# Narrow input columns of two mixers as four-group fp32 products, step sizes with tokens on the partitions

## What is computed

```
n = rmsnorm(h, norm_mix_w)
proj = n @ w_in                      # 1024 x (2*256 + 512 + 16 + 512 + 512 + 768 + 8)
q, k, v, gate_lr, g_out, z, xbc, dt_raw = split_cols(proj)
# gla: log_a = log_sigmoid(gate_lr @ w_gate2 + b_gate) / 16, sums over chunks of 64 tokens
# ssd: dt = softplus(dt_raw + dt_bias);  a = dt * -exp(a_log)
#      a_cum = cumsum(a) over chunks of 128 tokens; 8 heads
```

## Time and profile before

| | before |
|---|---|
| median of 3 runs | 2532.28 us (2531.97 to 2532.74) |
| the profiled execution's own time | 2532.24 us |
| its span, first to last instruction | 2530.5 us |
| TensorE busy | 2520.5 us of the span |
| DVE, ACT, POOL busy | 1617.3, 1035.7, 1002.1 us |

### The profile page before, as it was taken

How to read it: one execution, slowest core, us unless ns; L and a number is a source line. 1 busy time by engine, 2 the same in 40 slices (tenths; PEclk the granted TensorE clock), 3 DMA queues, 4 the chain that set the end, 5 groups by cost and what they waited for, 6 DMA issues and landing times.

```text
span 2530.5 us, 35784 instructions
## 1 busy us (share of the span) xinstructions
PE 2520.5 (100%) x13674; PEld 2196.4 (87%) x13674; DVE 1617.3 (64%) x3033; ACT 1035.7 (41%) x1621; POOL 1002.1 (40%) x545
## 2 busy tenths in 40 slices
PE   9999999999999999999999999999999999999999
PEld 7789899999999988888888888888889877988888
DVE  6746989899999978888888656610216275730112
ACT  6644344444444433333333534522324365542332
POOL 3324344535555523333332054444441424254442
PEclk9999999999999999999999999999999999999999
DMA  4313255789999999999999332223322322232331
GB/s 157 128 59 109 92 154 161 220 271 359 393 404 405 327 325 343 360 349 350 356 345 348 131 113 87 92 92 100 96 96 74 126 84 69 74 117 92 99 100 59
DMA packets 192907, 488.35 MB, mean 193 GB/s; under 512 B 18505, under 2 KB 83929, under 8 KB 192481
## 3 DMA queue, kind: packets, MB, share of 16 engines
q1 hardware_dynamic: 155872, 351.83, 41.6%
q0 software_dynamic: 36864, 134.23, 14.1%
HBM read 442.98 MB, written 42.88 MB: 192 GB/s over the span
## 4 chain that ended last, share of the span: by engine, by line
PE 91%; DVE 5%; DMA 2%; ACT 1%; POOL 1%; issue 1%; SPq 0%; DVEq 0%; ACTq 0%; POOLq 0%
PE ps L311 29%; PE ps L313 28%; PE ps L312 28%; PE ps L1750 1%; DVE wl L300 1%; DMA tmpb<-in_un,idx 1%; DMA rsb<-in_un,idx 1%; PE ps L2771 1%; PE ps L2868 1%; PE ps L1560 1%; PE ps L2831 1%; DVE tmpb L1879 1%; PE ps L525 0%; POOL wl L300 0%; ACT wh L292 0%
## 5 line engine op out<-in xcount | busy, mean ns | idle before, releaser
L292 ACT ACTIVATE wh<-wraw 128x1024 fp32r<-128x1024 f32 x487 | 514.0, 1058 | 1172.3 <-PE ps L313 1162.4
L300 POOL TENSOR_TENSOR wl<-wraw,wh 128x1024 fp32r<-128x1024 f32 x253 | 618.0, 2450 | 940.5 <-ACT wh L292 823.4
L311 PE MATMUL ps<-Xh,wh 128*128 128x384 f32 (+2 forms) x2336 | 828.9, 355 | 2.6 <-POOL wl L300 0.8
L313 PE MATMUL ps<-Xh,wl 128*128 128x384 f32 (+2 forms) x2336 | 817.5, 350 | 0.0
L312 PE MATMUL ps<-Xl,wh 128*128 128x384 f32 (+2 forms) x2336 | 817.2, 350 | 0.0
L311 PEld LDWEIGHTS ps<-Xh,wh 128*128 128x128 f32 x2336 | 439.7, 188 | 46.3 <-issue 5.5
L313 PEld LDWEIGHTS ps<-Xh,wl 128*128 128x128 f32 x2336 | 439.6, 188 | 38.7
L312 PEld LDWEIGHTS ps<-Xl,wh 128*128 128x128 f32 x2336 | 440.2, 188 | 36.2
L300 DVE TENSOR_TENSOR wl<-wraw,wh 128x1024 fp32r<-128x1024 f32 x234 | 286.0, 1223 | 82.2 <-ACT wh L292 78.9
L311 PE MATMUL ps<-wh,Hh 128*128 128x512 f32 x768 | 299.0, 389 | 0.0
L313 PE MATMUL ps<-wh,Hl 128*128 128x512 f32 x768 | 298.8, 389 | 0.0
(11 more groups left out here) (328 smaller groups left out, 3010.2 us busy)
## 6 DMA issues: line engine op xcount, KB each, us to landing
wraw<-in_uT SPq DMA_DIRECT2D x128, 512.0 KB
wraw<-in_v SPq DMA_DIRECT2D x128, 512.0 KB
wraw<-in_up SPq DMA_DIRECT2D x128, 512.0 KB
gA_scratch<-gl SPq DMA_DIRECT2D x122, 192.0 KB
gl<-gA_scratch SPq DMA_DIRECT2D x122, 192.0 KB
gG_scratch<-gbuf SPq DMA_DIRECT2D x64, 256.0 KB
lg<-gG_scratch SPq DMA_DIRECT2D x64, 256.0 KB
wraw<-in_w_q SPq DMA_DIRECT2D x24, 512.0 KB
```

Source lines behind the costliest of these rows:

```text
L292: act.activation(wh[:, n % 4, :], wraw[:, n % 4, :], ACT.Copy).then_inc(s_wh, 1)
L300: pool.tensor_tensor(wl[:, n % 4, :], wraw[:, n % 4, :], wh[:, n % 4, :].bitcast(F32), ALU.subtract).then_inc(s_wl, 1)
L311: pe.matmul(o, ah, bh, start=start, stop=False)
L313: return pe.matmul(o, al, bh, start=False, stop=stop)
```

## The change

- The narrow tile leaves the weights (`w_in` has one tile less, so that all tile numbers fall by one). Its 24 columns, padded to 32, come as a table `w_misc` of 128 x 256 with 16 more columns for the bias and a_log. POOL multiplies it by the norm's weight (`wm`). `misc_pe` makes 8 plain fp32 products of 32 columns against `hT`, chunk kc into partitions 32 (kc % 4) and following of bank 0: four column groups, each with two chunks. Two of them come among the first products, six after tile 3.
- The four groups are added in the next product: `w_gate2` is laid out four times (128 x 256), so that the gate product over 128 partitions sums them; `sel` is the identity's columns summed over the groups, so that `dt_pe` sums them and turns dt_raw at once to 128 tokens by 4 x 8.
- The chain of the step sizes runs on 128 x 32 elements. Running sums are products with a triangular matrix, the chunk totals one with ones (`decay_sums_pe`); the 4 scans, 8 transposes and the broadcast product go.
- The start is reordered: x in parts of 1, 1, 3, 3 chunks, the first ahead of `vec`, the first weight tile split in halves, 10 products of ones in place of 19.
- The order changes: project(4) stands between `root_pe` and `spread_pe`, project(5) right behind it, then `dt_pe` and the gate products; `decay_sums_pe` stands between tiles 7 and 8. In ACT's loop of six, split 9+i stands ahead of `silu_act(i)` where it stood behind `conv_act(i+2)`.

```
-    w2 = dg[:, 0:256]
+    w2, sel = dg[:, 0:256], dg[:, 256:264]
+    wm = Ss[:, 0, :].rearrange("p (c m) -> p c m", m=32)
+    y = dtt[:, :, :]
+    adt = GE[:, 2, 32:64]
     def in_sp(sp):
+        for i, (lo, hi) in enumerate(X_PARTS):
+            sp.dma_start(hT[:, lo:hi, :], xt[:, lo:hi, :]).then_inc(s_x[i], 16)
+            if i == 0:
+                sp.dma_start(vec[:, :], A["vec"]).then_inc(s_vec, 16)
+                load_w(sp, 0)
+            if i == 1:
+                load_w(sp, 1)
+                sp.dma_start(Ss[:, 0:2, :]..., A["w_misc"]).then_inc(s_small, 16)
+                load_w(sp, 2)
         load_w(sp, 3)
+        sp.wait_ge(s_small, 16)
+        sp.dma_start(w2, A["w_gate2"]).then_inc(s_small, 16)
-        sp.wait_ge(s_dt, 12)
-        sp.dma_start(acD, acT).then_inc(s_acd, 16)
+        sp.wait_ge(s_sd, 1)
+        sp.dma_start(acD32, acT_[:, :]).then_inc(s_acd, 16)
     def in_pool(pool):
+        pool.wait_ge(s_vec, 16)
+        pool.wait_ge(s_small, 16)
+        pool.tensor_tensor(wm, wm, mix, ALU.mult).then_inc(s_const, 1)
+    def misc_pe(pe, kcs):
+        for kc in kcs:
+            j = 32 * (kc % 4)
+            pe.wait_ge(s_x[X_PART[kc]], 16)
+            mm = pe.matmul(ps[B_INA[0]][j:j + 32, :], wm[:, kc, :], hT[:, kc, :], start=kc < 4, stop=kc >= 4)
+        return mm
+    def dt_pe(pe):
+        pe.wait_ge(s_in, 1)
+        for tc in range(4):
+            mm = pe.matmul(ps[6][:, tc * 8:tc * 8 + 8], misc[:, tc * 128:(tc + 1) * 128], sel, start=True, stop=True)
+        mm.then_inc(s_mp, 1)
+    def decay_sums_pe(pe):
+        pe.wait_ge(s_dt, 8)
+        b, by_tok = AUX["sp"], adt.rearrange("p (h c) -> p c h", c=4)
+        bank_free(pe, b)
+        pe.matmul(ps[b][0:32, 128:256], adt, tri[:, :], start=True, stop=True)
+        pe.matmul(ps[b][:, 0:32], tri[:, :], by_tok, start=True, stop=True).then_inc(s_sp, 1)
+        b = AUX["acl"]
+        pe.matmul(ps[b][:, 0:32], ones[:, :], by_tok, start=True, stop=True).then_inc(s_sp, 1)
     def in_pe(pe):
-        for i in range(19):
+        for i in range(10):
             pe.matmul(ps[7][:, 0:128], ones[:, :], ones[:, :], start=True, stop=True)
-        for c, gs in ((0, (0, 1)), (1, (0, 1)), (0, (2,)), (1, (2,)), *((c, (0, 1, 2)) for c in range(2, 8))):
+        for c, gs in ((0, (1,)), (1, (1,)), (0, ()), (0, (2,)), (1, (2,)), (0, (3,)), (1, (3,)), *((c, (1, 2, 3)) for c in range(2, 8))):
+            if not gs:
+                misc_pe(pe, MISC_FIRST)
+        misc_pe(pe, MISC_REST).then_inc(s_mp, 1)
+        freed[B_INA[0]] = done_in(0)
         root_pe(pe, "in", 5)
-        project(3)
+        project(4)
         spread_pe(pe, "in", 6, (s_kept, 1))
-        project(4)
-        ...
         project(5)
+        dt_pe(pe)
+        gate_lr_pe(pe)
         project(6)
         project(7)
+        decay_sums_pe(pe)
         project(8)
-        turn_dt_pe(pe)
         project(9)
         project(10)
-        last_sums_pe(pe)
         turn_b_pe(pe)
     def in_act(act):
             if c == 0:
-                split_hi(act, 0)
+                act.activation(wh[:, 0, 0:512], wraw[:, 0, 0:512], ACT.Copy).then_inc(s_w0, 1)
+                act.activation(wh[:, 0, 512:1024], wraw[:, 0, 512:1024], ACT.Copy).then_inc(s_wh, 1)
         for i in range(6):
+            if i < 4:
+                split_hi(act, 9 + i)
             silu_act(act, i)
             if i < 4:
                 conv_act(act, i + 2)
-                split_hi(act, 10 + i)
     def in_dve(dve):
+        dve.wait_ge(s_mp, 1)
         scaled(dve, misc, B_INA[0])
-        dve.tensor_scalar(y, y, col("dtb", 0, 0, 8), None, ALU.add).then_inc(s_dt, 1)
         xbc_dve(dve, 0)
         xbc_dve(dve, 1)
+        dve.wait_ge(s_mp, 2)
+        dve.tensor_tensor(y, ps[6][:, 0:32]..., dtb..., ALU.add).then_inc(s_dt, 1)
         dve.wait_ge(s_dta, 2)
         dve.tensor_scalar(u1, z, 1.0, None, ALU.add).then_inc(s_dt, 1)
         conv_dve(dve, 0)
         ...
-        dve.tensor_scalar(z, y, ea1[:, 0:1], -1.0, ALU.mult, ALU.mult).then_inc(s_dt, 1)
-        for c in range(4):
-            dve.tensor_tensor_scan(acT[:, cs], ones[0:8, :], z[:, cs], 0.0, ALU.mult, ALU.add).then_inc(s_dt, 1)
+        dve.scalar_tensor_tensor(out=adt..., in0=y, scalar=-1.0, in1=ea1..., op0=ALU.mult, op1=ALU.mult).then_inc(s_dt, 1)
         conv_dve(dve, 1)
         xbc_dve(dve, 3)
+        dve.wait_ge(s_sp, 1)
+        dve.tensor_copy(acT_[:, :], ps[AUX["sp"]][0:32, 128:256]).then_inc(s_sd, 1)
+        dve.tensor_copy(act_[:, :, :], ps[AUX["sp"]][:, 0:32]...).then_inc(s_sd, 1)
```

More of the change, by code:

```diff
@@ L129, in build_program @@
     zs = sb("zs", [128, 4, T], scope=mixer)
-    acT_ = sb("acT", [8, T], scope=mixer)
-    ea1 = sb("ea1", [8, 1], scope=mixer)
+    acT_ = sb("acT", [32, 128], scope=mixer)
+    ea1 = sb("ea1", [128, 8], scope=mixer)
     tri = sb("tri", [128, 128], scope=mixer)
@@ L672, in in_sp @@
     def in_sp(sp):
-        sp.dma_start(vec[:, :], A["vec"]).then_inc(s_vec, 16)
-        for i in range(4):
+        for i, (lo, hi) in enumerate(X_PARTS):
[3 more added lines that the diff above has]
+                load_w(sp, 0)
             if i == 1:
-                for n in range(3):
-                    load_w(sp, n)
-            sp.dma_start(hT[:, 2 * i:2 * i + 2, :], xt[:, 2 * i:2 * i + 2, :]).then_inc(s_x[i], 16)
+                load_w(sp, 1)
+                sp.dma_start(Ss[:, 0:2, :].rearrange("p a t -> p (a t)")[:, 0:272], A["w_misc"]).then_inc(s_small, 16)
+                load_w(sp, 2)
         load_w(sp, 3)
-        sp.dma_start(w2[32:48, :], A["w_gate2"]).then_inc(s_w2, 16)
-        for n in range(4, 13):
+        sp.wait_ge(s_small, 16)
+        sp.dma_start(w2, A["w_gate2"]).then_inc(s_small, 16)
+        for n in range(4, 12):
             load_w(sp, n)
-        sp.wait_ge(s_dt, 12)
-        sp.dma_start(acD, acT).then_inc(s_acd, 16)
+        sp.wait_ge(s_sd, 1)
+        sp.dma_start(acD32, acT_[:, :]).then_inc(s_acd, 16)
         sp.wait_ge(s_acd, ACD[0])
@@ L690, in in_sp @@
             lt_load(sp, h)
-        for n in range(13, 19):
+        for n in range(12, 18):
             load_w(sp, n)
@@ L697, in in_sp @@
             lt_load(sp, 2 * m + 1)
-            load_w(sp, 17 + m)
-        for n in range(21, W_OUT + 4):
+            load_w(sp, 16 + m)
+        for n in range(20, W_OUT + 4):
             load_w(sp, n)
     def in_pool(pool):
+        pool.wait_ge(s_vec, 16)
+        pool.wait_ge(s_small, 16)
+        mix = vec[:, COLS["mix"]:COLS["mix"] + 8].unsqueeze(2).to_broadcast([128, 8, 32])
+        pool.tensor_tensor(wm, wm, mix, ALU.mult).then_inc(s_const, 1)
         masks_pool(pool)
-        for n in range(4, 11):
+        pool.wait_ge(s_const, C_IDENT)
+        pool.tensor_tensor(sel, ident[:, 0:8], ident[:, 32:40], ALU.add).then_inc(s_const, 1)
+        for j in (2, 3):
+            pool.wait_ge(s_const, C_LEPS + j - 1)
+            pool.tensor_tensor(sel, sel, ident[:, 32 * j:32 * j + 8], ALU.add).then_inc(s_const, 1)
+        for n in range(4, 10):
             split_lo(pool, n)
         pool.wait_ge(s_sd, 1)
-        for n in range(11, 16):
+        for n in range(10, 15):
             split_lo(pool, n)
         pool.wait_ge(s_kp, 4)
-        for n in range(16, 22):
+        for n in range(15, 21):
             split_lo(pool, n)
@@ L1024, in in_act @@
             sum_square(act, "in", c, hT[:, c, :])
-        for n in range(4, 7):
+        for n in range(4, 6):
             split_hi(act, n)
         root_act(act, "in", 5, 1.0 / 1024)
-        split_hi(act, 7)
+        split_hi(act, 6)
         act.wait_ge(s_dt, 1)
@@ L1032, in in_act @@
         act.activation(z, z, ACT.Exp, scale=-1.0).then_inc(s_dta, 1)
-        act.activation(ea1[:, :], col("alog", 0, 0, 8), ACT.Exp).then_inc(s_dta, 1)
+        act.activation(ea1[:, :], alog, ACT.Exp).then_inc(s_dta, 1)
         conv_act(act, 0)
         conv_act(act, 1)
-        split_hi(act, 8)
+        split_hi(act, 7)
         for m in range(2):
@@ L1099, in in_act @@
         lt_act(act, 7)
+        split_hi(act, 19)
+        z_act(act, 1)
         split_hi(act, 20)
-        z_act(act, 1)
+        z_act(act, 2)
         split_hi(act, 21)
-        z_act(act, 2)
-        split_hi(act, 22)
         z_act(act, 3)
@@ L1555, in score_pe @@
         if m == 0:
[L1556 removed]
+            pe.wait_ge(s_small, 48)
         bank_free(pe, b)
@@ L3128, in _layout @@
     q, k, vv, gl, go, z, xbc, dt = (w[:, at[i]:at[i + 1]] for i in range(8))
-    misc = np.zeros((1024, 128), np.float32)
+    misc = np.zeros((1024, 32), np.float32)
     misc[:, 0:8] = dt
-    misc[:, 32:48] = gl
-    a["w_in"] = np.concatenate([_tiles(np.concatenate([misc, xbc[:, 512:], xbc[:, :512], q, k], 1)), _tiles_tok(vv),
+    misc[:, 8:24] = gl
+    rows = np.concatenate([v["ssd_dt_bias"][0], v["ssd_a_log"][0]])
+    a["w_misc"] = np.ascontiguousarray(np.concatenate([misc.reshape(8, 128, 32).transpose(1, 0, 2).reshape(128, 256),
```

(6 more changed lines are left out.)

131 lines of the change are left out of this document (64 added, 67 removed).

## The result

| | before | changed |
|---|---|---|
| median (range) | 2532.28 us (2531.97 to 2532.74, 7 runs) | 2540.73 us (2539.18 to 2541.38, 7 runs) |
| profiled execution, own time / span | 2532.24 / 2530.5 us | 2540.14 / 2538.4 us |

The ratio is 1.0031, with a 95% interval of 1.002 to 1.0042: slower, by 8.45 us or 0.3%. The forecast was no change, 2532.0 in a range up to 2536.3.

The account below looks back on a forecast made before the run. TensorE, busy 2520.5 of 2530.5 us, bounds the kernel. Terms between root and v sum to -2.0, with +1.3 at the start -0.7, with the clock -0.2: 2532.0 us, range 2529.3 to 2536.3.

Parts of the forecast that it names:

- the wait ahead of the sums: Before `decay_sums_pe`: TensorE due at 55.0, bank 4 freed by xbc(3) only at 56.3, so +1.3 us.
- The sum between root and v: From the first tiles' end (25.82) to the first v product (74.51): all terms together -2.0 us.
- My terms for that part: Narrow tile's products gone -5.43, `dt_pe` +0.95, three sum products +0.8, turn and its wait gone -1.2, old broadcast product -0.2.
- behind the spread: project(5) must wait for DVE's copy and scaling of the narrow result in bank 0: +1.75 us.
- +1.3 and 0.5: At the start: first tiles and narrow products end at 27.1 instead of 25.82, +1.3; clock possibly low, +0.5.
- the low clock there: At the start: +0.5 taken, between 0 and 1.4 us; the rival of a longer low clock, 2533.4 us, chance 0.2.
- the case without waits: Rival: the new waits don't bite and the clock rises, 2529.5 to 2530.5 us; range's lower end 2529.3; chance 0.15.
- the rival of two at a time: Narrow products: program order lets two column groups run at once, 4.4 us, +1.5, total 2533.5; chance 0.12.
- that of none: Narrow products: column groups don't run side by side, 7.2 us instead of 2.9, +4.3, total 2536.3; chance 0.08.
- The step sizes were ready: Before `decay_sums_pe`: the chain of step sizes ends at 53.3, in time for TensorE at 55.0.
- the rest shifts as a whole: Behind the first v product (74.51): untouched work waits for TensorE, so it moves as that point does.
- at most 0.5, taken as 0: ACT's splits ahead of silu: tile 12 lands near 70, conv(5) due at 73.5; cost at most 0.5 us.

Follow-up runs that it names:

- the run with products in the wait: Changed kernel with 24 products of ones ahead of `bank_free` in `decay_sums_pe`, filling TensorE's wait: 2538.43 us against 2540.73.
- The three last runs: Changed kernel with both banks moved, splits 8 and 9 on VectorE, narrow products together, ScalarE's old order: 2531.45 us; plus 17 products of ones: 2530.86; plus old transfers: 2530.07.
- the last run: Changed kernel with banks moved, splits 8 and 9 on VectorE, narrow products together, ScalarE's old order, 17 products of ones, old start transfers: 2530.07 us against 2532.14 before.

## Why the prediction was wrong

**The step that failed** is the price of the wait ahead of the sums: "But its bank 4 is freed by xbc(3), which DVE has behind conv(1): 2.28 + 0.69, so 56.3: **+1.3**." I costed VectorE's convolution at its length alone, and didn't ask what GpSimd does meanwhile. ScalarE's work for the step sizes and the gate holds back its splits 8 and 9 until 54.83. They come back to back, since in the changed order split 9 no longer has silu and conv_act in front of it, and so do GpSimd's, exactly beside conv(1). No run puts back ScalarE's order alone, so how much of the wait that would save is open. Measured: conv(1) took 6.29 us instead of 2.28, xbc(3) was done at 62.6, and the wait was 5.5 instead of 1.3. One wait on GpSimd brings it to 1.6. So the path that I named, bank 4 behind xbc(3), and its price without GpSimd were about right, and what I had left out is GpSimd beside VectorE.

**A term that was missing: the clock in the middle.** I looked for a low clock only at the start. The idle time behind 57 us brought it down, which cost 1.9 us by the run with products in the wait.

**The sum between root and v, term by term.** The three last runs have neither bank wait nor a low clock there, and take 43.52 us, 5.17 less than the kernel before. My terms for that part were -5.43 + 0.95 + 0.8 - 1.2 - 0.2 = -5.08. The changed kernel has three things on top, each read at the same two products in it and in the last run: 1.8 behind the spread (forecast 1.75), 5.6 ahead of the sums (forecast 1.3), 1.8 behind them, where the clock is low (forecast nothing). With -5.17 this is the measured +4.0, where I had -2.0.

**The start was mis-sized**, +3.6 instead of +1.3 and 0.5. The narrow products' last turns were right (1.85 us from 27.55 to 29.40, forecast 1.9). What stands ahead of them was not: the first tiles ended at 27.55 where I had 25.2. TensorE's first product came at 7.82 (forecast 7.1), and I had the landings too early: ScalarE takes up the second and third weight tile at 8.53 and 10.13 where I had 7.7 and 9.3, chunk 2 at 12.22 where I had 11.2.

```profile
8.53 1.06 ACT L295 ACTIVATE wh<-wraw 128x1024 fp32r<-128x1024 f32 x1 [0.44 <-DMA wraw<-in_w_in]
10.13 1.06 ACT L295 ACTIVATE wh<-wraw 128x1024 fp32r<-128x1024 f32 x1 [0.55 <-DMA wraw<-in_w_in]
12.22 1.95 ACT L595 ACTIVATE Xh<-hT,vec 128x512 fp32r<-128x512 f32 x3 [1.03 <-DMA hT<-in_xT]
```

I had scaled bytes by a rate taken between two landings. Undoing the transfers gave 0.9 us, putting the narrow products together 0.5, and the low clock there, which I priced at up to 1.4, gave 0.2 in one run and was worth more only where it lasted longer. With all three the root is at 27.68, which is 1.9 us, the eight narrow products, behind the kernel before.

**Two figures** were off without consequence: "the case without waits" comes to 2529.2 by its own terms, not 2529.3 or 2529.5, and the first x chunk with vec is some 325 KB by the page's sizes, not 321.

**What held.** The product behind the spread moved by 1.8 us (1.75 forecast), of which 1.5 are a wait. The four column groups run side by side: eight products in two turns, 1.92 us; the rival of two at a time (4.4 us) and that of none (7.2) are out, so the order in which products start and end did not hold back the next group. `dt_pe` took 0.8 us, from 43.56 to 44.37 (0.95 forecast). The step sizes were ready at 55.7, 1.6 us before TensorE came for them; the forecast was 1.7. That the rest shifts as a whole: 7.6 at v, 7.9 at the end. ScalarE's splits ahead of silu, "at most 0.5, taken as 0", were covered by the larger wait in the changed kernel; once that was gone they cost 2.2 us, four times my bound.

**The size of the expected gain.** The narrow tile's 5.43 us do go, and the products in its place cost 1.9. They were given back by order, not by arithmetic: with banks, splits and transfers put right, the median of the same change is 2.1 us below that of the kernel before, with an interval that just reaches no change.

## What to carry to other kernels

When a step moves, price what it delays on every engine by the operations that will then lie beside it: a VectorE operation with two SBUF inputs beside a GpSimd pass cost about the whole of that pass, 2.7 us instead of 0.75, and one with a single tensor as input seems to have been held as well (1.99 us instead of 0.41). A wait taken from a bank only moves on as long as the engine that frees banks is late; look for the engine, not for the bank. And a TensorE wait can be dearer than its length: the one of 5.5 us cost 1.9 more, since the clock fell in it.

## What the runs showed of the hardware

- fp32 products of 32 columns in four column groups: eight with 512 tokens took 1.92 us, where one takes 0.86 by the gate products.
- VectorE's scalar_tensor_tensor of 128 x 510 beside GpSimd's tensor_tensor of 128 x 1024 ended 0.5 us after GpSimd in both cases here, whenever it started; a tensor_scalar of 8 x 512 ended 0.3 us after it.
- The granted clock fell to half behind a wait of 1.6 us in two runs and after one of 2.2 us in a third, for 3.4 us each; with waits of 5.5 and 6.3 us it stayed low for 6.8 us, in one run for 10.2. Behind the wait of 1.5 us that ends at 38 us it fell in none of the runs that have it. What decides between 1.5 and 1.6 us was not tested.
- The runs of the changed kernel spread over 2.2 us, those of the kernel before over 0.8. The low stretches of the clock lay differently in the profiled executions; that they make the spread is likely, but was not shown.
